# A four-layer hybrid encoder trunk on one core: reciprocal-root chains and group preparation on GpSimd, side steps held back by engine load, two weight rings of six slots in place of three of four

## The reference

```
mem_n = rmsnorm(mem, mem_norm)
for i in range(4):
    h = rmsnorm(x, norm_mix[i])
    proj = h @ w_in            # 1024 x 7200 (SSM), 4096 (attention), 3072 (SGU)
    mix_out = mixer(proj[..., :-1024])
    cross = memory_cross_attention(proj[..., -1024:], mem_n, w_mem_kv[i], ...)
    x = x + concat(mix_out, cross) @ w_out
    x = x + square(relu(rmsnorm(x, norm_ffn[i]) @ w_ff1[i])) @ w_ff2[i]
rmsnorm(x, g) = x * rsqrt(mean(x*x) + 1e-6) * g
```

## Time and profile before

| | us |
|---|---|
| median of 3 runs | 1979.53 |
| lowest, highest | 1979.35, 1982.76 |
| the profiled execution: its own time | 1980.6 |
| the profiled execution: span of its instructions | 1978.7 |
| PE busy in that span | 1849.6 |
| DVE, ACT, POOL busy | 1057.8, 1009.5, 696.3 |

### The profile page before, as it was taken

One profiled execution on the slowest core, in us unless ns is written; L12 is line 12 of the kernel. 1 busy time (PEld: TensorE's weight loads), 2 busy tenths in 40 slices (PEclk: granted clock), 3 DMA queues, 4 the chain that ended last, 5 costly groups with the idle time before them and its releaser, 6 DMA issues.

```text
span 1978.7 us, 30229 instructions
## 1 busy us (share of the span) xinstructions
PE 1849.6 (93%) x10596; PEld 1611.3 (81%) x10596; DVE 1057.8 (53%) x1732; ACT 1009.5 (51%) x1616; POOL 696.3 (35%) x289
## 2 busy tenths in 40 slices
PE   6898888999999877999999999999989988999999
PEld 5787777899987656899988778999888876779997
DVE  6666756443337776443337643433666675644333
ACT  5555554454445545454446554544556564545443
POOL 3332221344443221344444323444333332134443
PEclk9999999999999988999999999999999999999999
DMA  6443332456554323355555435565544333255653
GB/s 214 142 142 117 107 118 96 150 181 192 189 185 158 118 99 115 129 180 193 189 186 195 153 118 180 181 192 192 160 158 151 128 117 107 96 161 180 192 187 133
DMA packets 84154, 305.72 MB, mean 155 GB/s; under 512 B 9280, under 2 KB 9664, under 8 KB 84032
## 3 DMA queue, kind: packets, MB, share of 16 engines
q1 hardware_dynamic: 83744, 302.95, 46.8%
q10 hardware_dynamic: 288, 1.05, 0.2%
HBM read 302.91 MB, written 1.05 MB: 154 GB/s over the span
## 4 chain that ended last, share of the span: by engine, by line
issue 44%; PE 37%; POOL 10%; DVE 6%; ACT 2%; POOLq 1%; DVEq 0%; ACTq 0%
POOL w_lo_t L843 10%; PE ps L892 7%; PE ps L893 7%; PE ps L894 7%; PE ps L901 4%; PE ps L903 4%; PE ps L902 4%; PE ps L955 1%; DVE mv L1409 1%; PE ps L1047 1%; PE ps L918 1%; PE ps L977 1%; DVE stats L1276 1%; DVE stats L1274 1%; PE ps L1027 1%
## 5 line engine op out<-in xcount | busy, mean ns | idle before, releaser
L843 POOL TENSOR_TENSOR w_lo_t<-raw,w_hi_t 128x1024 fp32r<-128x1024 f32 x285 | 696.1, 2443 | 1267.5 <-ACT w_hi_t L1072 1267.4
L1072 ACT ACTIVATE w_hi_t<-raw 128x1024 fp32r<-128x1024 f32 x570 | 599.5, 1060 | 432.9 <-PE ps L894 205.9
L1295 DVE TENSOR_TENSOR w_lo_t<-raw,w_hi_t 128x1024 fp32r<-128x1024 f32 x285 | 372.2, 1309 | 531.2 <-ACT w_hi_t L1072 530.3
L901 PE MATMUL ps<-hT_hi,w_hi_t 128*128 128x256 f32 x1536 | 440.4, 287 | 14.0 <-issue 14.0
L902 PE MATMUL ps<-hT_lo,w_hi_t 128*128 128x256 f32 x1536 | 436.4, 284 | 0.0
L903 PE MATMUL ps<-hT_hi,w_lo_t 128*128 128x256 f32 x1536 | 436.4, 284 | 0.0
L892 PE MATMUL ps<-w_hi_t,act_hi 128*128 128x512 f32 x832 | 327.4, 394 | 0.0
L893 PE MATMUL ps<-w_lo_t,act_hi 128*128 128x512 f32 x832 | 324.1, 390 | 0.0
L894 PE MATMUL ps<-w_hi_t,act_lo 128*128 128x512 f32 x832 | 323.9, 389 | 0.0
L901 PEld LDWEIGHTS ps<-hT_hi,w_hi_t 128*128 128x128 f32 x1536 | 296.7, 193 | 15.8 <-issue 14.4
L902 PEld LDWEIGHTS ps<-hT_lo,w_hi_t 128*128 128x128 f32 x1536 | 296.8, 193 | 1.3
(11 more groups left out here) (190 smaller groups left out, 2018.8 us busy)
## 6 DMA issues: line engine op xcount, KB each, us to landing
raw<-in_wstream SPq DMA_DIRECT2D x570, 512.0 KB, 3.4
mix<-in_mem SPq DMA_DIRECT2D x1, 1024.0 KB, 5.3
x<-in_x SPq DMA_DIRECT2D x1, 1024.0 KB, 10.7
out<-x SPq DMA_DIRECT2D x2, 512.0 KB, 2.8
wsT<-in_sgu_wT ACTq DMA_DIRECT2D x1, 512.0 KB, 3.6
sgain<-in_sgu_gain ACTq DMA_DIRECT2D x1, 512.0 KB, 4.5
consts_sb<-in_consts SPq DMA_DIRECT2D x1, 384.0 KB, 11.2
percol_sb<-in_percol SPq DMA_DIRECT2D x1, 225.5 KB, 6.5
```

Of the source, the lines that this page charges most:

```text
L843: return pool.tensor_tensor(w_lo_t[:, slot, :], raw[:, slot, :], w_hi_t[:, slot, :].bitcast(F32), ALU.subtract)
L901: pe.matmul(o, wh[:, n], ah, start=first and c == 0 and f % 2 == 0, stop=False, skip_group_check=True)
L1072: act.activation(w_hi_t[:, u % RING, :], raw[:, u % RING, :], ACT.Copy).then_inc(w_hi, 1)
L1295: dve.tensor_tensor(w_lo_t[:, u % RING, :], raw[:, u % RING, :], w_hi_t[:, u % RING, :].bitcast(F32), ALU.subtract)\
```

## The change

1. The plan's side threads may name the next step (`yield 1, "ssd_b"`). Each step kind has a cost for ACT, DVE and PE in a table; a running load of ACT and DVE is kept, and a named step is held back while an engine that it uses has more than `LATE` = 2.0 us of load. The exponentials become steps of their own (`d_exp`, `x_exp`), and the delays between steps are other ones.
2. The `rsqrt` chains of `rms`, the row norms (`norm_r`) and `group_r` run on POOL, as 14 dependent instructions; the four norms of a whole row ahead of a feed-forward block stay on DVE (`rms_ffn`). `ssd_prep` runs on POOL, without `xw`, which goes to `ssd_m` on DVE; `xdt` has two buffers.
3. POOL makes low parts only while `shared` is set (SSM layers from the dt unit on, the attention layer), alternating with DVE and in two halves of 512 columns; otherwise DVE makes them all: 121 on POOL and 449 on DVE.
4. The low part is written over the raw unit, and the two rings that are left have six slots; splits are made up to unit w + 4. A unit's load must now wait until PE has used unit u - 6.
5. The dt unit gets a side bank (`misc_job`), and an accumulator pair is not handed out before the plan has placed its last reader. ACT does one copy at the start, before the first data are awaited.

```
-RING = 4
+RING = 6
+AHEAD = 5
...
+LATE = 2.0
...
     def stream_job(self, act, dve):
         self.pair ^= 1
-        return Job(self, (2 * self.pair, 2 * self.pair + 1), act, dve)
+        banks = (2 * self.pair, 2 * self.pair + 1)
+        self.until(lambda: all(b not in self.last or self.last[b].is_read() for b in banks))
+        return Job(self, banks, act, dve)
...
+    def is_late(self, kind):
+        if kind is None:
+            return False
+        return any(c and self.load[e] > LATE for e, c in enumerate(COST[kind][:2]))
+
+    def advance(self, entry, early=False):
+        while entry[0] <= 0 and (early or not self.is_late(entry[3])):
...
+    def low_part_on(self, u):
+
+        return u % 2 if self.shared else 1
...
         def rest():
+            n = self.count("norm_r")
+            if groups != 2:
+                yield 1
+                self.step("norm_red", job=job, groups=groups, n=self.count("norm_red"))
+                self.step("norm_r", job=job, groups=groups, n=n, red=self.n["norm_red"])
+            else:
+                self.step("norm_r", job=job, groups=groups, n=n, red=0)
+                yield 1
             yield 1
             job.read_dve(self)
-            self.step("norm_mul", job=job, groups=groups, r=r)
-            yield 3
+            self.step("norm_mul", job=job, groups=groups, r=r, n=n)
+            yield 1
...
         r = self.rms("x")
         n = self.count("xn")
+        yield 1
         self.step("xn", n=n, rms=r)
-        yield 4
+        yield 1
...
-        job = self.stream_job(False, True)
+        self.shared = True
+        job = self.misc_job(False, True, read=False)
...
+        def prepare(g, done):
+            while g // 2 not in xs_act or self.decay_act is None:
+                yield 1
+            self.step("ssd_prep", g=g, l=l, n=l * SG + g, xs=xs_act[g // 2], done=done)
+            ready[g] = True
...
+                if g + 1 < SG:
+                    self.spawn(prepare(g + 1, jobs["S", 1].done), 1)
+                yield 1, "ssd_m"
+                self.step("ssd_m", g=g, n=n, jobs=jobs, decay=self.decay_act)
+                yield 2, "ssd_b"
...
-            with sp.Fori(1, NU // RING) as it:
...
+            for u in range(RING, NU):
+                kind, value = plan.release[u - RING]
+                sp.wait_ge(w_used if kind == "used" else job_done, value)
+                sp.dma_start(raw[:, u % RING, :], A["wstream"][u]).then_inc(raw_in[u % RING], 16)
...
+            def rsqrt(y, total, width):
+
+                n = total.shape[-1]
+                m, b = ta[:, 0:n], tb[:, 0:n]
+                link(pool.tensor_scalar(m, total, 1.0 / width, EPS, ALU.mult, ALU.add))
+                link(pool.tensor_scalar(y.bitcast(I32), m.bitcast(I32), -0.5, RSQRT_SEED, ALU.mult, ALU.add))
+                for k in range(3):
+                    link(pool.tensor_tensor(b, m, y, ALU.mult))
+                    link(pool.tensor_tensor(b, b, y, ALU.mult))
+                    link(pool.tensor_scalar(b, b, -0.5, 1.5, ALU.mult, ALU.add))
+                    ins = pool.tensor_tensor(y, y, b, ALU.mult)
+                    if k < 2:
+                        link(ins)
+                return ins
...
+                elif k == "norm_r":
+                    n = TT * s["groups"] if s["groups"] != 2 else 4
+                    if s["red"]:
+                        pool.wait_ge(red_new, s["red"])
+                    else:
+                        pool.wait_ge(act_free, s["job"].act)
+                    rsqrt(r_nt[:, 0:n], ssn[:, 0:n], COLS // s["groups"]).then_inc(rn_new, 1)
```

More of the change, by code:

```diff
@@ L62 @@
 NCN = CN["sgu_mask"] + 128
+COST = {
+    "turn": (0.85, 0.9, 0.45), "nt_turn": (0.85, 0, 0.45), "norm_sq": (1.9, 0, 0), "norm_red": (0, 1.2, 0), "norm_r": (0, 0, 0), "norm_mul": (0, 1.45, 0),
+    "evac": (1.2, 0, 0), "conv": (1.0, 2.7, 0), "silu": (1.1, 0, 0), "xs_turn": (1.2, 0, 0.9), "dt": (0, 0.4, 0), "dt_turn": (0.3, 0.7, 0.2),
+    "dt_soft": (0, 4.0, 0), "decay": (0.3, 0, 0.4), "ssd_prep": (0, 0, 0), "ssd_a": (1.5, 0.6, 2.25), "ssd_m": (0, 1.8, 0), "ssd_b": (0.4, 0.85, 2.15),
+    "ssd_o": (0, 1.7, 0.43), "yg_square": (1.2, 0, 0), "group_scale": (0.8, 0, 0), "d_score": (0, 2.6, 1.3), "d_exp": (2.0, 0, 0), "d_norm": (0, 1.9, 0),
+    "d_turn": (0.5, 0, 0.34), "d_av": (1.2, 0, 0.64), "o_scale": (0, 1.4, 0), "x_score": (0, 0.7, 1.72), "x_exp": (1.3, 0, 0), "x_norm": (0, 0.9, 0),
+    "x_turn": (0.6, 0, 0.45), "x_out": (0.6, 0.7, 1.72), "relu2": (1.3, 1.5, 0), "ff_split": (1.06, 1.23, 0), "ssq": (1.5, 0, 0), "xn": (0, 1.5, 0),
+    "x_add": (0, 1.5, 0), "sgu_sq": (1.2, 0, 0), "sgu_red": (0, 1.2, 0), "sgu_scale": (0, 1.0, 0), "sgu_mix": (0, 1.0, 0.86), "sgu_mask": (0, 1.2, 0),
+}
+LATE = 2.0
 class Job:
@@ L143, in spawn @@
     def spawn(self, thread, delay=0):
-        entry = [delay, thread, len(self.units)]
+        entry = [delay, thread, len(self.units), None]
         self.threads.append(entry)
@@ L155, in advance @@
                 return
+            entry[0], entry[3] = said if isinstance(said, tuple) else (said, None)
     def tick(self, early=False):
@@ L209, in rms, with rms_ffn @@
         return n
+    def rms_ffn(self):
+        n = self.count("rms_ffn")
+        self.step("rms_ffn", n=n, ssq=self.n["ssq"])
     def row_norm(self, job, groups, r, dst, tile, gain):
@@ L351, in rest @@
             self.misc = (4, 5, 6, 7)
-            for nb in range(2):
-                self.sum_squares("x", nb, self.x_halves[nb])
+            self.sum_squares("x", 0, a.dve)
             yield 1
-            self.r_x = self.rms("ffn" if gain[0] == "norm_ffn" else "x")
+            self.sum_squares("x", 1, b.dve)
+            if gain[0] == "norm_ffn":
+                yield 1
+                self.rms_ffn()
+            else:
+                self.rms("x")
         def scale_first(i):
@@ L518, in ssm @@
                 if k == 0:
-                    self.spawn(groups(), 4)
+                    self.spawn(groups(), 2)
             elif what == "q":
@@ L622, in squares @@
                 n = self.count("gn")
-                self.step("group_r", what=SGU, n=n, first=0, count=16, squares=None)
+                self.step("group_r", what=SGU, n=n, first=0, count=16, squares=("sg_red", 2))
+                yield 1
                 for t in range(TT):
                     for nb in range(2):
-                        yield 1
+                        yield 1, "sgu_scale"
                         self.step("sgu_scale", t=t, nb=nb, gn=n, last=t == 1 and nb == 1)
@@ L841, in _ @@
         def _(pool):
[L842 to L851 removed]
+            links = [0]
@@ new lines, in _, with link @@
+            low = [0]
+            def link(ins):
+                links[0] += 1
+                ins.then_inc(pool_chain, 1)
+                pool.wait_ge(pool_chain, links[0])
+            def rsqrt(y, total, width):
[11 more added lines that the diff above has]
+                return ins
@@ new lines, in over, with heads, lo_to @@
+            def over(a, groups, width):
+                return a.unsqueeze(2).to_broadcast([P, groups, width])
+            def heads(a, n=HPG):
+                return a.rearrange("p (h c) -> p h c", h=n)
+            def lo_to(n):
+                while low[0] < min(n, NU):
+                    u = low[0]
+                    if plan.lo_on[u] == 0:
+                        pool.wait_ge(w_hi, u + 1)
+                        for h in range(2):
+                            c = slice(h * COLS, (h + 1) * COLS)
+                            ins = pool.tensor_tensor(w_lo_t[:, u % RING, c], raw[:, u % RING, c], w_hi_t[:, u % RING, c].bitcast(F32), ALU.subtract)
+                        ins.then_inc(w_lo[0], 1)
+                    low[0] += 1
@@ L1096, in _ @@
                 elif k == "ssq":
+                    sums = ss_mem if s["src"] == "mem" else ss_x
                     if s["src"] == "mem":
```

312 lines of the change are left out of this document (170 added, 142 removed).

## The result

The changed kernel takes 1890.4 us (median of 4 runs, 1888.3 to 1893.8) against 1979.4 us (4 runs, 1975.7 to 1982.8): a ratio of 0.955, 95% interval 0.953 to 0.958. 1888 was predicted. The profiled execution has a span of 1886.3 us. The two errors offset each other.

What follows compares the result with a forecast made beforehand. The prediction took the kernel to be bound by PE, with its idle time and clock loss to win. From 1980.6 us, -95 (side steps), -26 (clock) and +28 (new waits) gave 1888 us, range 1841 to 1945 at 0.8.

Steps and rivals of the forecast that it cites:

- The nine waits: Nine rows of PE waiting at side steps whose partner engine has not finished, 95 us in all, predicted to go.
- Part 1: Side steps in the mixers are moved to new distances, so PE's waits for them go: -95 us.
- New waits: +28 us: PE waits added by chains on POOL, at row norms, ahead of layer 3 and at the start: +28 us.
- 14.0 us for the bank: First SSM unit's wait for its accumulator bank, predicted to go with the dt unit's side bank: 14.0 us.
- Part 2: PE's low clock in the mixers: at most 50 us to win back, half taken, -26 us.
- Part 3: Chains on POOL: 14 links at 0.30 us, 5.5 us a chain with blocking; new waits +28 us.
- 22 places: 20 norms and two `xn` with a transposition behind them without room; each further us of chain costs 22 us.
- Two-group norms: 16 norms of 2 groups: PE waits 1.6 us where nothing else stands between; 5 us counted in all.
- Part 4: Low parts and rings: feed-forward low parts on DVE stay hidden and loads keep 6.6 us of cover; worth zero.
- (a): Rival: the waits move to other steps and half of the idle-time and clock gains comes back, 1948 us; chance 0.13.
- (b): Rival: chains on POOL too slow; gain gone at 0.60 us a link, 2027 us at 0.75; chance 0.08.
- (c): Rival: loads on demand make PE stand for each of 570 units, 2002 us at 0.2 us each; chance 0.04.

Runs made afterwards that it cites:

- the early reduction: Changed kernel with the reduction of the attention layer's four 8-group norms one unit earlier, in the gap of ACT's squares: 1879.2 us, ratio 0.9497.

## Why the prediction was right, step by step

**The sum.** Predicted -95 - 26 + 28 = -93 us, measured -64.0 of idle and -28.4 of busy time, -92.4. That it comes out so closely is luck in three places. The nine waits fell by 15 us less than they should, and some 16 us of smaller waits that no part named went away. The new waits have nearly the foreseen sum by other terms. And the half of the clock's bound was a choice.

**What bounds it, and the pace.** Right: all of the gain lies in the mixers, in the idle time and the clock.

**Part 1, -95 us.** Nearly right as a size: the nine waits fell by 79.6 us. Wrong in what it takes: I wrote that the steps' new places make these waits go, and held the chains' move for a separate cost. With the same places and the chains on DVE the time is 1934 to 1944, so about half of the gain hangs on the move. The step that failed is "New waits: +28 us" as a price of POOL: measured against the alternative in the same order, POOL's chains are worth 39 to 53 us. Only in the old order, where the run above has it 15 us slower, is the move a cost. I had compared a chain's length on the two engines, 2.4 against 5.5 us, and not what is queued behind it, and the 2.4 was wrong, too: 4.42 on average against 4.93. On POOL nothing but low parts, needed units later, stands behind it; on DVE it is the whole of the side work.

**Its 14.0 us for the bank** measured 8.5 in the new order, 6.4 of it in PE's idle time.

**Part 2, -26 us.** PE's busy time fell by 28.4 us. The half that I took was a choice between 0 and 50; no run shows why a half.

**Part 3, the chain.** Predicted 0.30 a link and 5.5 us a chain, measured 0.28 and 4.93. The blocking of "one or two" low parts was 1.3 meetings of 0.8 us each. 22 us for each us of chain: the figure came out with the longer chain, but by fewer and longer waits than 22 places, and a third of it is the clock. Downward the prediction had counted with less than half of this price, 13 us for 1.3 us of blocking; no run made a chain shorter.

**The new waits, +28 us.** 31.3 over the kernel before, 36.3 in the rows, by other terms. *Layer 1*: 16 counted; of the 16.0 in the row, 14.1 are there. But I put them on ACT's squares and the chain; the early reduction takes 8 of them with the chain untouched, so more than half is the reduction's place behind the scores. *Two-group norms*: 5 counted, 1.9 seen. *Ahead of layer 3*: 5 counted, 4.5 seen (14.8 less 10.3). *Start*: 2 counted, 10.3 seen. I saw two chains in a row; there are three, the first met three low parts (7.0 us), and the one for x is last. *Decay product*: 0 counted, 5.5 seen; I had not looked at what the dt step's place makes late.

**Part 4, zero.** Right for the low parts in the feed-forward blocks, and right that 6.6 us of cover suffice: no wait of PE for a low part behind the first unit. Taking two slots away costs 42 us, so the zero holds only with the six slots under the new loading rule; what they would be worth in the kernel before no run shows. For the sharing of low parts in layer 2 the run leaves -2 to 9 us.

**The rivals.** (a) didn't come: 60 us did not return. (b) was real as a mechanism and off in size: 0.28 us a link, not 0.60. In the old order the move did turn the time slower, at this same 0.28, for a reason that rival (b) left out: DVE standing inside one gap for POOL, which makes a low part first. (c) appears with four slots, in 22 places and not in 570.

## What to carry to other kernels

Ask of a dependent chain not which engine runs it fastest but what stands behind it in that engine's order, and whether its inputs are ready when the engine gets there. Here a slower engine with little in its order won when the order left a gap between input, chain and use; the move without the new order lost 15 us, and the new order without the move gave about half. After such a move look for the first consumer: a reduction one place behind a stranger's step cost 11 us here, and with it a needed chain queued third, a scaled copy and a decay product placed too early, all mended by small edits, 26 us. The chain queued third gave nothing that can be told when mended alone.

## What was not expected of the hardware

A 14-link chain of operations on 2 to 16 columns was only 16% shorter on DVE than on POOL (4.14 against 4.93 us), because each link of 0.17 us that meets a half low part of POOL becomes one of 1.2 us. In the kernel before, where POOL's low part was one instruction, the same meeting cost 2.31 us, and a 12-link chain took 4.42: halving the long instruction on one engine halved the stall on the other.

The mean clock of a stretch changes with nothing edited in it and the same waits. Layer 1 of the changed kernel, with 21.3 us of idle PE, has 0.99 and 223.3 us of busy PE; in the run with the other start order, 21.3 us and 0.97, 225.8; in the run with dt on a stream bank, 21.4 us and 0.96, 227.6; in the run with rings of four, 21.0 us and 0.99, 223.5. These are single executions, and the runs don't settle what decides it. A gain of under 5 us at one place can't be read from one profile.
